# Expert weights with four rows (two for the down matrix) on one partition, and stationary tiles read with a step

## The reference

```python
a = jax.nn.silu(jnp.einsum('nd,edf->nef', x, w_gate)) * jnp.einsum('nd,edf->nef', x, w_up)
y = jnp.einsum('nef,efd->nd', a * gates[..., None].astype(a.dtype), w_down)
```

## Time and profile before

| | |
|---|---|
| median of 3 runs | 1386.2 us (1379.71 to 1386.77) |
| profiled execution | 1377.41 us |
| its span, first to last instruction | 1375.6 us |
| mean granted TensorE clock | 0.950 |
| TensorE matmul, weight loads | busy 1225.5 us (89%), 626.7 us (46%) |
| VectorE, ScalarE, GpSimd | busy 404.6 us (29%), 233.0 us (17%), 40.9 us (3%) |
| moved by DMA | 315.11 MB in 138885 packets, mean 229 GB/s |
| chain that ended last | TensorE 78%, DMA 10%, VectorE 7% |

### The profile page before, as it was taken

One profiled execution on the slowest core, in us unless ns is written; L12 is line 12 of the kernel. 1 busy time (PEld: TensorE's weight loads), 2 busy tenths in 40 slices (PEclk: granted clock), 3 DMA queues, 4 the chain that ended last, 5 costly groups with the idle time before them and its releaser, 6 DMA issues.

```text
span 1375.6 us, 15086 instructions
## 1 busy us (share of the span) xinstructions
PE 1225.5 (89%) x6172; PEld 626.7 (46%) x6172; DVE 404.6 (29%) x1154; ACT 233.0 (17%) x487; POOL 40.9 (3%) x64
## 2 busy tenths in 40 slices
PE   3899989897879999998879998989787899999985
PEld 3445546684453243433434554558445234343343
DVE  1511031453351223222351203136334122322234
ACT  1210121231130010100031012124112001010002
POOL 1500000000020000000000000000000000000000
PEclk9999999998989999999999999999898999999998
DMA  9945333755319999999551543341430999999931
GB/s 351 302 142 199 135 119 123 258 202 108 122 37 377 395 377 385 387 385 393 196 184 61 202 173 122 123 160 55 108 122 0 340 395 385 383 392 387 393 135 46
DMA packets 138885, 315.11 MB, mean 229 GB/s; under 512 B 5964, under 2 KB 6208, under 8 KB 138688
## 3 DMA queue, kind: packets, MB, share of 16 engines
q1 hardware_dynamic: 135232, 306.43, 61.3%
q0 software_dynamic: 3584, 7.71, 2.2%
HBM read 310.92 MB, written 4.99 MB: 230 GB/s over the span
## 4 chain that ended last, share of the span: by engine, by line
PE 78%; DMA 10%; DVE 7%; ACT 2%; issue 2%; SPq 1%; DVEq 0%; ACTq 0%
PE ps L813 14%; PE ps L1077 13%; DMA ring<-in_w_up 8%; PE ps L823 8%; PE ps L991 6%; PE ps L1112 6%; PE ps L1060 6%; PE ps L1036 5%; PE ps L773 3%; PE ps L790 2%; PE ps L1138 1%; DMA ring<-in_w_mod 1%; PE ps L930 1%; PE ps L1001 1%; PE ps L803 1%
## 5 line engine op out<-in xcount | busy, mean ns | idle before, releaser
L1077 PE MATMUL ps<-ring,arena 128*64 128x512 f32 x832 | 242.8, 605 | 13.1 <-DMA ring<-in_w_up 13.1
L1677 DVE SCALAR_TENSOR_TENSOR xT<-ps,modT,xT 128x128 f32<-128x128 f32 x320 | 115.5, 412 | 297.7 <-PE ps L1060 208.3
L813 PE MATMUL ps<-ring,hT 128*128 128x512 f32 (+1 forms) x480 | 197.7, 571 | 0.0
L813 PEld LDWEIGHTS ps<-ring,hT 128*128 128x128 f32 x480 | 91.6, 192 | 99.9 <-issue 96.8
L1077 PEld LDWEIGHTS ps<-ring,arena 128*64 128x64 f32 x832 | 67.0, 137 | 130.6 <-issue 130.6
L1112 PE MATMUL ps<-ring,arena 128*64 128x512 f32 x384 | 115.0, 605 | 8.3 <-ACT arena L1380 8.3
L1060 PE MATMUL ps<-hT 128*128 128x384 f32 x256 | 110.9, 529 | 2.8 <-issue 1.7
L823 PE MATMUL ps<-hT,ring 128*128 128x384 f32 x320 | 106.2, 489 | 0.0
L1077 PE MATMUL ps<-slot,arena 128*64 128x512 f32 x192 | 94.5, 600 | 1.4 <-issue 1.4
L991 PE MATMUL ps<-mixT,ring 128*128 128x384 f32 x256 | 88.0, 509 | 1.7 <-ACT mixT L1353 1.7
L1060 PEld LDWEIGHTS ps<-hT 128*128 128x128 f32 x256 | 39.4, 188 | 94.1 <-issue 82.9
(11 more groups left out here) (301 smaller groups left out, 1196.0 us busy)
## 6 DMA issues: line engine op xcount, KB each, us to landing
ring<-in_w_up SPq DMA_DIRECT2D x56, 1024.0 KB, 10.3
ring<-in_w_gate SPq DMA_DIRECT2D x54, 1024.0 KB, 14.1
ring<-in_w_down SPq DMA_DIRECT2D x50, 1024.0 KB, 10.1
ring<-in_w_mod SPq DMA_DIRECT2D x24, 2048.0 KB, 12.4
ring<-in_w_in SPq DMA_DIRECT2D x14, 2048.0 KB, 9.0
slot<-in_w_down SPq DMA_DIRECT2D x18, 1024.0 KB, 12.3
slot<-in_w_gate SPq DMA_DIRECT2D x14, 1024.0 KB, 12.6
slot<-in_w_up SPq DMA_DIRECT2D x12, 1024.0 KB, 10.1
```

Source lines behind the costliest of these rows:

```text
L813: mm = pe.matmul(p[:, 0:n], hT[:, k, t * P:(t + 1) * P], w[:, k, c0:c0 + n], start=(k == 0), stop=(k == KT - 1))
L1077: mm = pe.matmul(out[which][64 * s:64 * s + 64, :], xg[:, k, cols[s]], w[i][:, k % 4, :], start=(k == 0), stop=(k == KT - 1))
L1677: ins = dve.scalar_tensor_tensor(xT[:, m, cols], p[:, cols], modT[:, L, gate0 + m, j:j + 1], xT[:, m, cols], ALU.mult, ALU.add)
```

## The change

The rows of a chunk are laid out on the partitions in another way. A gate or up chunk puts four neighbouring rows on a partition: partition p holds rows 4p to 4p + 3 of its 512, which is one run of 8192 bytes in memory. A down chunk puts two rows on a partition: rows 2p and 2p + 1 of its 256, again 8192 bytes. Buffers, chunk sizes, order and waits are as before.

With that, tile `r` of a gate or up chunk holds the rows 4p + r. The other operand must have the same features on the same partitions, so the gather takes the columns `r`, `r + 4`, `r + 8`, ... of its half of `h2_high` and `h2_low` (a step of 16 bytes) where it took 128 neighbouring ones, and the transposes of `act_in` take every second column of a half (a step of 8 bytes). `interleaved` gives these slices. Each engine has the same instructions in the same order with the same shapes.

```diff
+FEATURE_RUN = 4
+
+
+def interleaved(k, run):
+
+    first = k // run * run * P + k % run
+    return slice(first, first + (P - 1) * run + 1, run)
+
...
                     kt = (FF // P if which == "D" else KT) // 2
                     w = a[{"G": "w_gate", "U": "w_up", "D": "w_down"}[which]][ly.number]
-                    sp.dma_start(slots[slot].rearrange("p (k n) -> p k n", k=kt),
+                    run = 2 if which == "D" else FEATURE_RUN
+                    sp.dma_start(slots[slot].rearrange("p (k n) -> p k n", k=kt // run),
                                  w[bass.ds(expert, 1), upper * kt * P:(upper + 1) * kt * P
-                                   ].rearrange("e (k p) n -> p (e k) n", p=P)).then_inc(ly.chunk_loaded[slot], 16)
+                                   ].rearrange("e (k p r) n -> p (e k) (r n)", p=P, r=run)
+                                 ).then_inc(ly.chunk_loaded[slot], 16)
...
                             for part in (h2_high, h2_low):
-                                mm = pe.matmul(out, part[:, t, k * P:(k + 1) * P], selected[t],
+                                mm = pe.matmul(out, part[:, t, interleaved(k, FEATURE_RUN)], selected[t],
                                                start=(t == 0 and part is h2_high), stop=(t == 2 and part is h2_low))
...
                     for f in range(4):
-                        mm = pe.transpose(p[:, f * P:(f + 1) * P], act_in[:, f * P:(f + 1) * P], ident)
+                        mm = pe.transpose(p[:, f * P:(f + 1) * P], act_in[:, interleaved(f, 2)], ident)
...
                     for f in range(4):
-                        mm = pe.transpose(p[:, f * P:(f + 1) * P], act_in[:, f * P:(f + 1) * P], ident)
+                        mm = pe.transpose(p[:, f * P:(f + 1) * P], act_in[:, interleaved(f, 2)], ident)
```

## The result

The changed kernel takes 1401.36 us in the median of four runs (1397.84 to 1405.27), the kernel before 1384.78 us in four; the ratio is 1.013, with a 95% interval of 1.0094 to 1.0166. It is slower by some 17 us. I had forecast 1371. The case that came is the first rival, weight loads that slow down with the step, which I had put at 1400 with a chance of 0.24. The measured time lies 0.4 us above the upper end of the range.

A forecast was written before the change was run, and what follows sets the result against it. Expert stages were taken as bound by DMA and TensorE, both nearly full. Profiled 1377.4 us less 14.5 (16.5 recoverable, 2 staying), zero for strided reads, gave 1362.9; 8.8 up to the median scale made 1371.7, said as 1371; range 1361 to 1401.

The forecast's parts named there:

- the first rival: Gathers and overflow job: stepped weight loads run at half rate, 14 us slower, 1400 by the median; chance 0.24.
- What bounds the kernel: Expert stages: DMA and TensorE both nearly full; 18.2 us lost to stalls, 16.5 recoverable; the bound moves to TensorE.
- the plain pairs: Expert pairs without a gather, such as 5, 6, 7: 29.71 us on TensorE without a stall, 29.84 for their transfers.
- The transfers: Expert weight loads: 8192-byte runs take 310.8 ns at 422 GB/s; a pair's twelve loads fall from 31.99 to 29.84 us.
- The sum's 14.5 us: Forecast gain in the expert stages: 16.5 us recoverable less 2 us of waits that stay.
- The strided reads: Gathers and act_in transposes: stepped stationary loads cost nothing; far ends 43 us for gathers, 10 us for transposes.
- I take zero for both: Zero extra time for the stepped loads of the gathers and for those of the act_in transposes.
- The second zero: Act_in transposes at an 8-byte step: no extra time for 72 loads, at most 10 us.
- 288 loads: Weight loads, 144 per layer, in gathers of pairs 2 and 4 and the overflow job, without cover; at most 43 us.

The follow-up runs named there:

- the layout alone: New weight layout on the kernel before, with gathers and act_in transposes reading neighbouring columns, so products pair other features: 1365.84 us, ratio 0.9867.
- the run with the stepped identity: Changed kernel, but the gather reads neighbouring columns; the h2 transposes sort them by reading the identity at a 16-byte step: 1365.56 us, ratio 0.9888.
- the run with other steps: Kernel before with steps of 12 to 32 bytes in later gathers and 12 or 16 in act_in transposes: 1475.44 us, not comparable.
- two rows: Changed kernel with two neighbouring rows per partition for gate and up too, 4096-byte runs and an 8-byte gather step: 1370.67 us, ratio 0.9912.
- the steps alone: Kernel before, old weight layout, with only the stepped reads of gathers and act_in transposes added: 1417.39 us, ratio 1.0225.

## Why the prediction was wrong

- **What bounds the kernel: right.** Both engines were nearly full, and with faster transfers the plain pairs fell to TensorE's own 29.7 us.
- **The transfers: right, to the size.** 311 ns per run of 8192 bytes against 310.8, 421 GB/s against 422. The sum's 14.5 us lies inside what the layout alone gives: 12.8 us in the profile, 18 (13 to 23) by the ratio. The rule of the Trainium skill in "DMA: Bandwidth & Descriptors" (section "Why small descriptors are slow (HBM only)") would have given 3.5% more rate for gate and up; the windows show 421 against 386, which is 9%.
- **The strided reads: this step failed.** The sum said "I take zero for both". The gather's part was worth 2 x (11.5 + 4.9 to 5.4), some 33 us in two layers. The argument that carried it, that a load reads at half the pace of the other operand and so has room for a step, was a guess about a reader from the pace of another: the run with the stepped identity shows that the moving operand pays too, and the run with other steps shows what the price goes by, the count of 16-byte pieces at some 1.86 ns each. At 8 bytes 64 pieces take 119 ns by that price (125 measured), hardly more than a load needs anyway (111 to 118), so that step is nearly free; at 16 bytes 128 pieces take 238. The second zero held, though not by that count: the four transposes of a pair take 0.76 us where they took 0.67, and the plain pitch is 29.74 instead of 29.71 us.
- **The rival was right in place, and near in size**: its sum is 14 us, 17 were measured by the medians and 20.8 in the stretches from the first gather on. Its price was too low: half rate was taken as 222 ns per matmul, and 238 came. That the load ran near half rate at all is the count of pieces at 16 bytes; at 12 bytes it is 181 ns. The Trainium skill, "SBUF — State Buffer" (section "Door 1: The DMA port swizzle"), says that reads need two hits on a 16-byte line to keep their pace, and the traces agree: two hits (8 bytes) 125 ns, one hit (16 bytes) 238. Its sentence that four fp32 elements are a free step does not hold here.
- **The chances.** 288 loads stood open and nothing in the trace priced them. That was the larger unknown of the two, and 0.24 was too little for it; this is a judgement, no run shows a chance. The range ended at 1401, 1 us above the rival's own 1400, so the 16 ns that its price lacked per load (288 x 16 ns = 4.6 us) had no room.

## What to carry to other kernels

A longer run per partition raises the rate of a full DMA queue (386, 409, 421 GB/s at 2, 4 and 8 KB here), and that is worth time only until the compute engine is the bound: two rows gave 11.0 of the 12.8 us that the layout alone gives in the profiles. Before a tile is read with a step, look for the places where its read sets the pace, which are those where a matmul with fewer columns takes no less time, and keep two float32 elements in each 16 bytes. If the order of the columns has to change, change it where they are made, in the identity of a transpose that runs anyway, which cost nothing that could be measured here.

## What the runs showed of the hardware that was not expected

- The pace of the gather's stepped weight loads follows the number of 16-byte pieces, 1.8 to 1.95 ns each, and is flat from 16 to 32 bytes (226 to 245 ns for 128 columns). The loads of the act_in transposes do not follow it (0.76 us for four at 8 and at 16 bytes).
- That pace does not depend on TensorE's clock: 48 loads at 16 bytes take 11.42 us with a mean granted clock of 0.60 as at 1.00, while plain loads go from 111 to 213 ns at 0.50.
- The moving operand of a transpose pays too: 407 instead of 273 ns per record at 16 bytes, 230 instead of 111 from one to the next. ScalarE pays for a step of 512 bytes on its write to SBUF (1085 against 614 ns), VectorE for the same step on its write and on one of its reads (1024 against 683).
- A transpose with sorted columns in its identity and four separate blocks in its output is as fast as the plain one (273 ns).
- Longer gathers did not let the weights catch up: with the steps alone the waits for weights stayed at 13.0 us, because the ten buffers were full and the transfers fell to 130 GB/s in the 8 us behind the gather.
